# First attention of a two-block transformer kernel: values held stationary for two heads in the two column halves of the array, probabilities scaled ahead of their transposes

## The chip, the cores and the metric

The kernel runs on one core of a Trainium2 chip. The metric is the device time of one execution in microseconds (us). TensorE is the matrix engine: a matmul loads its stationary operand into a 128 x 128 array and streams the moving operand through it, a column at a time. VectorE (DVE in the profile), ScalarE (ACT) and GpSimd (POOL) are the other compute engines, each with an instruction stream of its own that is worked off in order; they meet at semaphores. SyncE (SP) issues the loads.

## The reference

The reference is two transformer blocks on 256 tokens of width 1024. The first block is a feed-forward part, a mixing part and a second feed-forward part; the second block has a differential attention, a recurrence and an MLP. What the change touches is the mixing part of the first block, in which two attentions of 8 heads of width 64 run side by side over the same normed input `u`:

```
qa, ka, va, qb, kb, vb, qi, ki, wi, g = jnp.split(u @ w_in[l], SPLIT_POINTS, axis=-1)
...
out_a = dsa_attention(qa, ka, va, qi, ki, wi, bias_dsa)
out_b = moba_attention(qb, kb, vb, bias_moba)
...
mixed = g_a * (out_a @ w_branch_dsa[l]) + g_b * (out_b @ w_branch_moba[l])
h = h + mixed @ w_out[l]
```

Both are causal softmax attentions with a bias by distance; with 256 tokens `moba_attention` has a single block and is plain causal attention. `dsa_attention` lets each query see only the 64 keys with the highest scores of a small index network:

```
_, idx = lax.top_k(scores, topk)
...
p = jax.nn.softmax(logits, axis=-1)
return jnp.einsum('bqhk,bqkhd->bqhd', p.astype(v.dtype), v_sel)
```

## The kernel before

Weights are streamed from memory in units of 128 x 4 x 512 numbers through a ring of three buffers. Each unit is split into two parts, `hi` (ScalarE, L721 for half a unit in this stage, L712 for a whole one elsewhere) and `lo` (VectorE, L1135 or L1118), and each product of activations and weights is done as three matmuls of 512 moving columns, at L1635 to L1637. A call of `portion` is four such threes, 12 matmuls.

The mixing part's input products are 11 chunks of columns (`IN1`), two units and two tiles of 128 tokens each, so 44 portions. The program counts them as positions p = 0 to 43, and each engine's instruction stream walks through the same positions in its own loop `for p in range(4 * len(IN1))`. Tables by position say where an engine fits in the attention's work: TensorE does the portion of position p and then the small matmuls that the tables put there. Of the table `M1_STEP` an entry is the position at which a head's logits are made, one step for each of 16 heads: steps k = 0 to 7 are the heads of the `moba` attention, 8 to 15 those of the `dsa` attention.

```
M1_STEP = [17, 19, 21, 22, 23, 24, 25, 26] + [29 + k for k in range(NH)]
```

For step k with s = M1_STEP[k]:

- TensorE at s, for even k: `pair_scores`, the scores of two heads, with their 64 rows of queries and keys in the upper and lower half of the array's rows (L1781 to L1785).
- VectorE at s: `logits` (L1258), which adds the bias and finds the maximum of each row, into `l1[:, k % 4]`. 384 columns: 256 keys for the second tile of queries, 128 for the first, since the first can't see later keys.
- ScalarE at s + 1: the exponential, with row sums (L929), semaphore `m_p`.
- TensorE at s + 3: three transposes of 128 x 128 into the bank `PT` (L1868), which wait for `m_p`.
- ScalarE at s + 3: the copy from `PT` to `pt1` (L897).
- TensorE at s + 4: the values product (L1882 to L1884), three matmuls with the transposed probabilities stationary and 64 columns of values moving.

When a branch's 8 heads are done, VectorE takes reciprocals of the sums and scales the outputs from the banks `O` into `hid` (L1426); TensorE then transposes them tile by tile at the positions `M1_OUT_T` (L1894), and ScalarE and VectorE split what comes out into `mth` and `mtl`, or `ath` and `atl` (L937, L1434), the stationary operands of the branch's output product.

Other work stands between these on VectorE. At each of the positions 13 to 20 it does an eighth of the search for the top keys (L1405 to L1408); at 21 the found keys become a mask (L1411). Queries and keys of the chunks 4 and 5 (positions 16 to 23) are normed: VectorE sums squares of each head (L1343, L1345), GpSimd takes the root (`head_rstd`, L633), VectorE scales (`head_scale`, L1351), one position after the sums, and TensorE transposes the result (L1837). GpSimd, after its last root, adds the mask to the `dsa` bias in one instruction (L650, `bias_a<-bias_a,score`). At each position VectorE ends with half a split (L1135).

## Time and profile before

| | |
|---|---|
| median of 3 runs | 1036.5 us (1035.03 to 1036.72) |
| the profiled execution | 1035.49 us |
| its span, first to last instruction | 1033.7 us |
| TensorE busy | 1021.1 us, 99% of the span |
| VectorE busy | 626.5 us, 61% |
| ScalarE busy | 544.6 us, 53% |
| GpSimd busy | 121.7 us, 12% |
| first attention, 250 to 356 us: TensorE, VectorE, ScalarE busy | 104.19, 76.35 and 63.30 us |

Times of rows are microseconds from the span's start. Matmuls are pipelined, so the time from the start of one to the start of the next is its price, not the duration in its row, which overlaps with the next one's.

### The profile page before, as it was taken

How to read it: one execution, taken by the hardware profiler on the slowest of the kernel's cores; microseconds unless marked ns; L12 is line 12 of the kernel's file. 1: busy time of each engine (PE TensorE's matmuls, PEld its weight loads, DVE VectorE, ACT ScalarE, POOL GpSimd, SP SyncE). 2: the span in 40 equal slices, each digit the busy share in tenths (PEclk: the TensorE clock that was granted, in tenths of full speed). 3: DMA queues.
4: the chain of work that ended last, by engine and by line, in shares of the span. 5: the costliest groups of instructions: out<-in, count | busy, mean ns of one | idle time of the engine just before them, and what ended most of it. 6: DMA issues, size and time to landing. Idle time of an engine off the chain costs nothing.

```text
span 1033.7 us, 13217 instructions
## 1 busy us (share of the span) xinstructions
PE 1021.1 (99%) x4854; PEld 840.3 (81%) x4854; DVE 626.5 (61%) x868; ACT 544.6 (53%) x745; POOL 121.7 (12%) x110
## 2 busy tenths in 40 slices
PE   8999999999999999999999999999999999999998
PEld 6788888888878888888888888888888888888886
DVE  5555454568875667554454667766498765454553
ACT  7344434565755636444434576766875555444441
POOL 0000000032310000000000041219913000000000
PEclk9999999999999999999999999999999999999999
DMA  7777665585433546656555366445355555555541
GB/s 248 240 242 241 203 232 188 161 295 181 143 122 124 172 153 204 202 166 201 175 191 192 134 248 206 151 135 163 122 188 197 185 163 198 174 199 175 190 162 41
DMA packets 113815, 188.83 MB, mean 183 GB/s; under 512 B 4577, under 2 KB 60010, under 8 KB 113642
## 3 DMA queue, kind: packets, MB, share of 16 engines
q1 hardware_dynamic: 113754, 188.23, 55.2%
q8 instruction: 28, 0.46, 0.2%
q14 instruction: 17, 0.14, 0.0%
q10 hardware_dynamic: 16, 0.00, 0.0%
HBM read 182.45 MB, written 5.77 MB: 182 GB/s over the span
## 4 chain that ended last, share of the span: by engine, by line
PE 91%; DVE 3%; ACT 2%; DMA 1%; POOL 1%; issue 1%; SPq 1%; DVEq 0%; ACTq 0%; POOLq 0%
PE bank L1635 21%; PE bank L1637 21%; PE bank L1636 21%; PE bank L1730 7%; PE bank L1729 7%; PE bank L1731 6%; PE bank L1674 2%; PE bank L1647 1%; PE bank L1781 1%; DVE hid L1351 1%; ACT hi L712 1%; DVE lo L1135 1%; POOL rstd_q L633 1%; PE bank L1971 1%; DMA resid<-in_x 1%
## 5 line engine op out<-in xcount | busy, mean ns | idle before, releaser
L1635 PE MATMUL bank<-hi,xh 128*128 128x512 f32 (+1 forms) x944 | 378.2, 401 | 2.4 <-DVE hid L1171 0.8
L1637 PE MATMUL bank<-hi,xl 128*128 128x512 f32 (+1 forms) x944 | 368.1, 390 | 0.0
L1636 PE MATMUL bank<-lo,xh 128*128 128x512 f32 (+1 forms) x944 | 366.6, 388 | 0.0
L1118 DVE TENSOR_TENSOR lo<-raw,hi 128x2048 fp32r<-128x2048 f32 x112 | 255.9, 2286 | 174.5 <-ACT hi L712 174.4
L712 ACT ACTIVATE hi<-raw 128x2048 fp32r<-128x2048 f32 (+1 forms) x116 | 220.6, 1903 | 141.7 <-PE bank L1731 98.6
L1635 PEld LDWEIGHTS bank<-hi,xh 128*128 128x128 f32 x944 | 177.4, 188 | 39.9 <-DVE xl L1157 1.8
L1637 PEld LDWEIGHTS bank<-hi,xl 128*128 128x128 f32 x944 | 177.2, 188 | 37.9
L1636 PEld LDWEIGHTS bank<-lo,xh 128*128 128x128 f32 x944 | 177.7, 188 | 33.6
L1135 DVE TENSOR_TENSOR lo<-raw,hi 128x1024 fp32r<-128x1024 f32 (+1 forms) x108 | 133.2, 1242 | 53.6 <-ACT hi L721 53.0
L1729 PE MATMUL bank<-hi,hh 128*128 128x512 f32 x304 | 119.7, 394 | 1.1 <-DVE hl L1181 1.1
L1730 PE MATMUL bank<-lo,hh 128*128 128x512 f32 x304 | 119.7, 394 | 0.0
L1731 PE MATMUL bank<-hi,hl 128*128 128x512 f32 x304 | 118.2, 389 | 0.0
L721 ACT ACTIVATE hi<-raw 128x1024 fp32r<-128x1024 f32 x100 | 104.0, 1050 | 13.1 <-PE bank L1637 9.9
L789 ACT ACTIVATE hh<-bank 128x512 fp32r<-128x512 f32 x38 | 21.9, 597 | 115.2 <-PE bank L1674 115.2
L1729 PEld LDWEIGHTS bank<-hi,hh 128*128 128x128 f32 x304 | 57.1, 188 | 14.1 <-issue 1.3
L1731 PEld LDWEIGHTS bank<-hi,hl 128*128 128x128 f32 x304 | 57.1, 188 | 12.8
L1181 DVE TENSOR_TENSOR hl<-bank,hh 128x512 fp32r<-128x512 f32 x38 | 25.5, 688 | 68.8 <-ACT hh L789 68.8
L1730 PEld LDWEIGHTS bank<-lo,hh 128*128 128x128 f32 x304 | 57.2, 188 | 11.3
L626 POOL TENSOR_TENSOR small<-small 128x1 f32<-128x1 f32 x10 | 8.2, 822 | 377.4 <-DVE small L1142 377.4
L633 POOL TENSOR_TENSOR rstd_q<-ss_q,small 128x8 f32<-128x8 f32 x16 | 37.8, 2362 | 92.5 <-DVE ss_q L1345 92.5
L778 ACT ACTIVATE act_out<-bank,small 128x256 f32<-128x256 f32 x44 | 20.8, 474 | 50.4 <-PE bank L1637 50.4
L1171 DVE SCALAR_TENSOR_TENSOR hid<-bank,small,act_out 128x256 f32<-128x256 f32 x44 | 21.1, 481 | 18.1 <-ACT act_out L778 18.1
(247 smaller groups left out, 941.3 us busy)
## 6 DMA issues: line engine op xcount, KB each, us to landing
raw<-in_w_in SPq DMA_DIRECT2D x48, 1024.0 KB
raw<-in_ffn_w_gu SPq DMA_DIRECT2D x84, 512.0 KB
raw<-in_ffn_w_down SPq DMA_DIRECT2D x22, 1024.0 KB
raw<-in_w_up SPq DMA_DIRECT2D x16, 1024.0 KB
raw<-in_w_down SPq DMA_DIRECT2D x16, 1024.0 KB
raw<-in_w_out SPq DMA_DIRECT2D x8, 1024.0 KB
distance_table<-ftab SPq DMA_DIRECT2D x8, 576.0 KB
raw<-in_w_proj_attn SPq DMA_DIRECT2D x4, 1024.0 KB
```

The source lines that it names most:

```text
L633: nc.gpsimd.tensor_tensor(rstd_q[:, s], ss_q[:, s], minus_half[:, 0:8], ALU.pow).then_inc(rstd_sem, 1)
L712: nc.scalar.activation(hi[s][:, :, 0:width], raw[s][:, :, 0:width], ACT.Copy).then_inc(hi_done, 1)
L721: ins = nc.scalar.activation(hi[s][:, cut, :], raw[s][:, cut, :], ACT.Copy)
L1118: nc.vector.tensor_tensor(lo[s][:, :, 0:width], raw[s][:, :, 0:width], hi[s][:, :, 0:width].bitcast(F32), ALU.subtract).then_inc(lo_done, 1)
L1135: ins = nc.vector.tensor_tensor(lo[s][:, cut, 0:width], raw[s][:, cut, 0:width], hi[s][:, cut, 0:width].bitcast(F32), ALU.subtract)
L1181: nc.vector.tensor_tensor(hl[:, kt:kt + 2, :], X[b][:, :].rearrange("p (k c) -> p k c", k=2), hh[:, kt:kt + 2, :].bitcast(F32), ALU.subtra ...
L1635: nc.tensor.matmul(o, sh, wh, start=first and j == 0, stop=False)
L1636: nc.tensor.matmul(o, sh, wl, start=False, stop=False)
L1637: ins = nc.tensor.matmul(o, sl, wh, start=False, stop=last and j == 3)
L1729: nc.tensor.matmul(DB[t][h][:, :], sh, wh, start=begin, stop=False)
L1730: nc.tensor.matmul(DB[t][h][:, :], sh, wl, start=False, stop=False)
L1731: ins = nc.tensor.matmul(DB[t][h][:, :], sl, wh, start=False, stop=end)
```

## The change

Three things change together. The probabilities of a step are scaled by their reciprocal sums in `l1`, by VectorE at position s + 2, ahead of the transposes, which now wait for that (semaphore `m_n`) and not for the exponential. The values product is done once for two heads (`pair_values`): a head's values, 64 columns, are stationary, one head in the left column half of the array and the other in the right, and the transposed probabilities move, 256 and 128 columns; it comes out with the features in the partitions, as the output product wants it. So the scaling and the transposes of outputs go, and ScalarE and VectorE split the outputs straight from the banks `O`, four heads at a time, at the positions `M1_OUT`. `pt1` has four buffers in place of two.

```diff
-M1_OUT_T = [32, 33, 42, 43]
+M1_OUT = [27, 31, 37, 41]
...
-            pt1 = sb("pt1", [P, 2, SPAN], F32, s)
+            pt1 = sb("pt1", [P, 4, SPAN], F32, s)
...
                     act.wait_ge(m_pt, k + 1)
-                    if k >= 2:
-                        act.wait_ge(m_pv, k - 1)
-                    nc.scalar.activation(pt1[:, k % 2, :], PT[:, 0:SPAN], ACT.Copy).then_inc(m_ptc, 1)
+                    if k >= 4:
+                        act.wait_ge(m_pv, k - 3)
+                    nc.scalar.activation(pt1[:, k % 4, :], PT[:, 0:SPAN], ACT.Copy).then_inc(m_ptc, 1)
...
-                j = at(M1_OUT_T, p)
+                j = at(M1_OUT, p)
                 if j >= 0:
-                    act.wait_ge(m_ot, j + 1)
+
+                    act.wait_ge(m_pv, 4 * (j + 1))
                     dst = mth if j < 2 else ath
-                    nc.scalar.activation(dst[:, :, j % 2 * P:(j % 2 + 1) * P],
-                                         X[0][:, :].rearrange("p (k c) -> p k c", c=P), ACT.Copy).then_inc(m_oh, 1)
+                    nc.scalar.activation(dst[:, 2 * (j % 2):2 * (j % 2) + 2, :],
+                                         O[j % 2][:, :].rearrange("p (k c) -> p k c", c=SEQ),
+                                         ACT.Copy).then_inc(m_oh, 1)
...
-                for branch in range(2):
-                    if M1_STEP[NH * branch + NH - 1] + 4 == p:
-
-                        dve.wait_ge(m_p, NH * (branch + 1))
-                        cut = slice(2 * NH * branch, 2 * NH * (branch + 1))
-                        step(nc.vector.reciprocal(inv[:, cut], sums[:, cut]))
-                        dve.wait_ge(m_pv, NH * (branch + 1))
-                        if branch == 0:
-                            dve.wait_ge(m_tr, 10)
-                        else:
-                            dve.wait_ge(m_ot, 2)
-                        for tt in range(NT):
-                            r = inv[:, cut].rearrange("p (h q) -> p h q", q=2)[:, :, 1 - tt:2 - tt]
-                            nc.vector.tensor_tensor(hid[:, tt, :].rearrange("p (h c) -> p h c", c=HD),
-                                                    O[tt][:, :].rearrange("p (h c) -> p h c", c=HD),
-                                                    r.to_broadcast([P, NH, HD]), ALU.mult).then_inc(m_o, 1)
-                j = at(M1_OUT_T, p)
+                k = at(M1_STEP, p - 2)
+                if k >= 0:
+
+                    dve.wait_ge(m_p, k + 1)
+                    step(nc.vector.reciprocal(inv[:, 2 * k:2 * k + 2], sums[:, 2 * k:2 * k + 2]))
+                    for q, cut in enumerate((slice(0, SEQ), slice(SEQ, SPAN))):
+                        ins = nc.vector.tensor_scalar(l1[:, k % 4, cut], l1[:, k % 4, cut],
+                                                      inv[:, 2 * k + q:2 * k + q + 1], None, ALU.mult)
+                    ins.then_inc(m_n, 1)
+                j = at(M1_OUT, p)
                 if j >= 0:
                     dve.wait_ge(m_oh, j + 1)
...
+            def pair_values(v, k):
+
+                h = k % NH
+                o = O[h // 4]
+                first = h // 2 % 2 * SEQ
+                whole, late = slice(first, first + SEQ), slice(first + P, first + SEQ)
+                left, right = slice(h * HD, h * HD + HD), slice(h * HD + HD, h * HD + 2 * HD)
+                one, two = pt1[:, k % 4, :], pt1[:, k % 4 + 1, :]
+                nc.tensor.matmul(o[0:HD, whole], v[:, 0, left], one[:, 0:SEQ], start=True, stop=False)
+                nc.tensor.matmul(o[HD:P, whole], v[:, 0, right], two[:, 0:SEQ], start=True, stop=False)
+                nc.tensor.matmul(o[0:HD, late], v[:, 1, left], one[:, SEQ:SPAN],
+                                 start=False, stop=True).then_inc(m_pv, 1)
+                nc.tensor.matmul(o[HD:P, late], v[:, 1, right], two[:, SEQ:SPAN],
+                                 start=False, stop=True).then_inc(m_pv, 1)
...
                 k = at(M1_STEP, p - 3)
                 if k >= 0:
 
-                    pe.wait_ge(m_p, k + 1)
+                    pe.wait_ge(m_n, k + 1)
                     if k >= 1:
                         pe.wait_ge(m_ptc, k)
-                    for j in range(3):
-                        ins = nc.tensor.transpose(PT[:, j * P:(j + 1) * P], l1[:, k % 4, j * P:(j + 1) * P],
+                    for j, b in enumerate((2, 0, 1)):
+                        ins = nc.tensor.transpose(PT[:, j * P:(j + 1) * P], l1[:, k % 4, b * P:(b + 1) * P],
                                                   ident[:, :])
                     ins.then_inc(m_pt, 1)
                 k = at(M1_STEP, p - 4)
-                if k >= 0:
+                if k >= 0 and k % 2 == 1:
+
                     pe.wait_ge(m_ptc, k + 1)
-                    if k == 0:
+                    if k == 1:
                         pe.wait_ge(m_ev, 8)
-                    if k == NH:
-                        pe.wait_ge(m_o, 2)
+                    if k == NH + 1:
                         pe.wait_ge(m_ev, 14)
...
+                    if k >= NH and k % 4 == 1:
+                        pe.wait_ge(m_ol, (k - NH) // 4 + 1)
+                    pair_values(v1 if k < NH else v1b, k - 1)
...
-                    if q == 2:
-                        pe.wait_ge(m_ol, 3 + t)
+                    if q in (0, 2) and t == 0:
+                        pe.wait_ge(m_ol, q + 2)
```

The order of instructions shows it at three places. On TensorE, behind the portion of position 21: the transposes of normed queries, the scores of two heads, and before the change the values product of step 0.

```order
L1837 MATMUL bank<-ident,hid 128x128 [waits m_qn,m_trev]
L1837 MATMUL bank<-ident,hid 128x128 x3
L1781 MATMUL bank<-k_m,q_m 128x256 [waits m_l]
L1782 MATMUL bank<-k_m,q_m 128x256
L1783 MATMUL bank<-k_m,q_m 128x128
L1785 MATMUL bank<-k_m,q_m 128x128
L1882 MATMUL bank<-v,pt 128x64 [waits m_ev,m_ptc]
L1883 MATMUL bank<-v,pt 128x64
L1884 MATMUL bank<-v,pt 128x64
```

After the change the first values product stands two positions later, behind the portion and the scores of position 23, and is that of the steps 0 and 1; its outputs are 64 partitions high (`64x256`, `64x128`).

```order
L1775 MATMUL bank<-k_m,q_m 128x256 [waits m_l]
L1776 MATMUL bank<-k_m,q_m 128x256
L1777 MATMUL bank<-k_m,q_m 128x128
L1779 MATMUL bank<-k_m,q_m 128x128
L1790 MATMUL bank<-pt,v 64x256 [waits m_ev,m_ptc]
L1791 MATMUL bank<-pt,v 64x256
L1792 MATMUL bank<-pt,v 64x128
L1794 MATMUL bank<-pt,v 64x128
```

So the single product went from position 21, and a pair's came at 23. The transposes of step 0, at position 20, stand where they stood, and wait for `m_n` in place of `m_p`.

On VectorE at position 19, with the end of the head sums, a part of the top-key search, and the split, before the change:

```order
L1345 TENSOR_SCALAR ss_q<-ss_q 128x8 [waits m_red]
L1405 MAX small<-score 128x8
L1406 MAX small<-score 128x8
L1407 MATCH_REPLACE score<-small,score 128x256 [waits dve_step]
L1408 MATCH_REPLACE score<-small,score 128x128
L1135 TENSOR_TENSOR lo<-raw,hi 128x1024 [waits hi_half,dve_step]
L1351 TENSOR_TENSOR hid<-hid,rstd_q 128x512 [waits m_rstd]
```

and after it:

```order
L1346 TENSOR_SCALAR ss_q<-ss_q 128x8 [waits m_red]
L1406 MAX small<-score 128x8
L1407 MAX small<-score 128x8
L1408 MATCH_REPLACE score<-small,score 128x256 [waits dve_step]
L1409 MATCH_REPLACE score<-small,score 128x128
L1418 RECIPROCAL small<-small 128x2 [waits m_p,dve_step]
L1420 TENSOR_SCALAR l<-l,small 128x256 [waits dve_step]
L1420 TENSOR_SCALAR l<-l,small 128x128
L1136 TENSOR_TENSOR lo<-raw,hi 128x1024 [waits hi_half]
L1352 TENSOR_TENSOR hid<-hid,rstd_q 128x512 [waits m_rstd]
```

The scaling of step 0 (L1418, L1420) stands between the search and the split.

On VectorE at position 24, where the logits of step 5 are followed by the last head scaling, before the change:

```order
L1262 TENSOR_SCALAR small<-small 128x2 [waits dve_step]
L1351 TENSOR_TENSOR hid<-hid,rstd_q 128x512 [waits m_rstd]
L1135 TENSOR_TENSOR lo<-raw,hi 128x1024 [waits hi_done]
L1258 ISA l,small<-bank,bias_m 128x256 [waits m_pt,m_s]
L1258 ISA small 128x1
```

and after it:

```order
L1263 TENSOR_SCALAR small<-small 128x2 [waits dve_step]
L1352 TENSOR_TENSOR hid<-hid,rstd_q 128x512 [waits m_rstd]
L1418 RECIPROCAL small<-small 128x2 [waits m_p]
L1420 TENSOR_SCALAR l<-l,small 128x256 [waits dve_step]
L1420 TENSOR_SCALAR l<-l,small 128x128
L1136 TENSOR_TENSOR lo<-raw,hi 128x1024 [waits hi_done]
L1259 ISA l,small<-bank,bias_m 128x256 [waits m_pt,m_s]
L1259 ISA small 128x1
```

The scaling of step 3 stands directly behind the head scaling. TensorE's transposes of step 3 are at position 25.

## Rows read from the trace of the kernel before

**Rows 1.** The page: TensorE's share of the span, and its granted clock in 40 slices.

```profile
PE 1021.1 (99%) x4854; PEld 840.3 (81%) x4854; DVE 626.5 (61%) x868; ACT 544.6 (53%) x745; POOL 121.7 (12%) x110
...
PEclk9999999999999999999999999999999999999999
```

**Rows 2.** TensorE's waits: line, releaser, us in total, times, longest.

```profile
PE bank L1837 <- DVE hid L1351: 1.8, 1, 1.8
```

**Rows 3.** Timeline of TensorE around a values product alone: start, duration, line, tiles.

```profile
345.23 0.39 PE L1637 MATMUL bank<-hi,xl 128*128 128x512 f32 x1
...
346.59 0.39 PE L1637 MATMUL bank<-hi,xl 128*128 128x512 f32 x1
```

**Rows 4.** The same around the transposes L1894 of an output tile.

```profile
351.36 0.40 PE L1637 MATMUL bank<-hi,xl 128*128 128x512 f32 x1
...
352.50 0.40 PE L1637 MATMUL bank<-hi,xl 128*128 128x512 f32 x1
```

**Rows 5.** The same around a scores product of two heads.

```profile
309.11 0.39 PE L1637 MATMUL bank<-hi,xl 128*128 128x512 f32 x1
309.42 0.48 PE L1781 MATMUL bank<-k_a,q_a 64*128 64x256 f32 x1
309.43 0.48 PE L1782 MATMUL bank<-k_a,q_a 64*128 64x256 f32 x1
...
309.96 0.27 PE L1783 MATMUL bank<-k_a,q_a 64*128 64x128 f32 x1
...
310.07 0.27 PE L1783 MATMUL bank<-k_a,q_a 64*128 64x128 f32 x1
...
310.85 0.40 PE L1637 MATMUL bank<-hi,xl 128*128 128x512 f32 x1
```

**Rows 6.** Timeline of ScalarE at position 18: the exponential of step 0.

```profile
260.54 0.51 ACT L929 ACTIVATE l<-l,small 128x256 f32<-128x256 f32 x1
```

**Rows 7.** Timeline of TensorE: transposes of steps 0, 2 and 3, then L1837.

```profile
263.12 0.49 PE L1868 MATMUL bank<-ident,l 128*128 128x128 f32 x3
...
279.13 0.49 PE L1868 MATMUL bank<-ident,l 128*128 128x128 f32 x3
...
283.60 0.55 PE L1868 MATMUL bank<-ident,l 128*128 128x128 f32 x3
...
289.40 0.63 PE L1837 MATMUL bank<-ident,hid 128*128 128x128 f32 x4 [1.81 <-DVE hid L1351]
```

**Rows 8.** Timeline of VectorE: splits of positions 19 and 22, then 23 and 24.

```profile
267.29 1.22 DVE L1135 TENSOR_TENSOR lo<-raw,hi 128x1024 fp32r<-128x1024 f32 x1
...
275.94 1.22 DVE L1135 TENSOR_TENSOR lo<-raw,hi 128x1024 fp32r<-128x1024 f32 x1 [0.56 <-ACT hi L721]
277.09 0.42 DVE L1258 CUSTOM_DVE_ANT_0 l<-bank,bias_m 128x256 f32<-128x256 f32 x1
...
277.83 0.68 DVE L1351 TENSOR_TENSOR hid<-hid,rstd_q 128x512 f32<-128x512 f32 x1
...
279.15 0.17 DVE L1345 TENSOR_SCALAR ss_q<-ss_q 128x8 f32<-128x8 f32 x1
...
281.97 7.28 DVE L1351 TENSOR_TENSOR hid<-hid,rstd_q 128x512 f32<-128x512 f32 x1 [0.77 <-POOL rstd_q L633]
```

**Rows 9.** Timeline of VectorE in the second attention: a reciprocal and two multiplications.

```profile
640.17 0.17 DVE L1508 RECIPROCAL small<-small 128x4 f32<-128x4 f32 x1
...
640.64 0.55 DVE L1513 TENSOR_SCALAR l<-l,small 128x256 f32<-128x256 f32 x2
```

**Rows 10.** Timeline of GpSimd: the last root of head sums and the mask addition.

```profile
279.40 2.54 POOL L633 TENSOR_TENSOR rstd_q<-ss_q,small 128x8 f32<-128x8 f32 x1 [2.30 <-DVE ss_q L1345]
281.91 6.79 POOL L650 TENSOR_TENSOR bias_a<-bias_a,score 128x3072 f32<-128x3072 f32 x1
```

**Rows 11.** Timeline of TensorE at the start of the trace, 0 to 14 us.

```profile
1.82 1.97 PE L1768 MATMUL bank<-ident 128*128 128x128 f32 x8 [1.82 <-POOL small L621]
...
5.67 2.35 PE L1768 MATMUL bank<-ident 128*128 128x128 f32 x20
```

More of the change, by code:

```diff
@@ L352, in program @@
         m_p = sem("m_p")
+        m_n = sem("m_n")
         m_pt = sem("m_pt")
@@ L355, in program @@
         m_pv = sem("m_pv")
-        m_o = sem("m_o")
-        m_ot = sem("m_ot")
         m_oh = sem("m_oh")
@@ L1432, in _ @@
                     hi_, lo_ = (mth, mtl) if j < 2 else (ath, atl)
-                    cut = slice(j % 2 * P, (j % 2 + 1) * P)
-                    nc.vector.tensor_tensor(lo_[:, :, cut], X[0][:, :].rearrange("p (k c) -> p k c", c=P),
-                                            hi_[:, :, cut].bitcast(F32), ALU.subtract).then_inc(m_ol, 1)
+                    cut = slice(2 * (j % 2), 2 * (j % 2) + 2)
+                    nc.vector.tensor_tensor(lo_[:, cut, :], O[j % 2][:, :].rearrange("p (k c) -> p k c", c=SEQ),
+                                            hi_[:, cut, :].bitcast(F32), ALU.subtract).then_inc(m_ol, 1)
                 mixing_split(split_lo_half, U_M1, p)
@@ L1871, in _ @@
                 k = at(M1_STEP, p - 4)
-                if k >= 0:
+                if k >= 0 and k % 2 == 1:
                     pe.wait_ge(m_ptc, k + 1)
-                    if k == 0:
+                    if k == 1:
                         pe.wait_ge(m_ev, 8)
-                    if k == NH:
-                        pe.wait_ge(m_o, 2)
+                    if k == NH + 1:
                         pe.wait_ge(m_ev, 14)
-                    h = k % NH
-                    v = v1 if k < NH else v1b
-                    cut = slice(h * HD, (h + 1) * HD)
-                    nc.tensor.matmul(O[1][:, cut], pt1[:, k % 2, 0:P], v[:, 0, cut], start=True, stop=False)
-                    nc.tensor.matmul(O[1][:, cut], pt1[:, k % 2, P:SEQ], v[:, 1, cut], start=False, stop=True)
-                    nc.tensor.matmul(O[0][:, cut], pt1[:, k % 2, SEQ:SPAN], v[:, 0, cut],
-                                     start=True, stop=True).then_inc(m_pv, 1)
-                j = at(M1_OUT_T, p)
-                if j >= 0:
-                    pe.wait_ge(m_o, j + 1)
-                    if j == 0:
-                        pe.wait_ge(m_trev, 10)
-                    else:
-                        pe.wait_ge(m_ol, j)
-                    for b in range(4):
-                        ins = nc.tensor.transpose(X[0][:, b * P:(b + 1) * P], hid[:, j % 2, b * P:(b + 1) * P],
-                                                  ident[:, :])
-                    ins.then_inc(m_ot, 1)
+                    if k >= NH and k % 4 == 1:
+                        pe.wait_ge(m_ol, (k - NH) // 4 + 1)
+                    pair_values(v1 if k < NH else v1b, k - 1)
             for q in range(4):
```

## The prediction

> **What bounds the kernel now.** The page says TensorE is busy for 99% of the span [rows 1], and its list of waits has only a few entries: 1.8 us is its wait in the first attention, the transposes at L1837 waiting for a VectorE instruction [rows 2]. So I read the first attention as a timeline of TensorE between 250 and 356 us, and beside it the timelines of VectorE, ScalarE and GpSimd. The reader should look for two things: what a small group of matmuls costs between two long ones, and when each small group would be ready to run under its new wait. As TensorE has nothing spare, every microsecond that it loses or saves in this stage should be in the end time.
>
> **Prices on TensorE.** Long matmuls follow each other every 0.227 us. Three of them, with the thing between, give each price. With one head's values: 345.23 to 346.59 is 1.36, less 0.68 for the three, 0.68 us a head [rows 3]. With four transposes of outputs: 351.36 to 352.50 is 1.14, so 0.46 [rows 4].
>
> The new values product, one for a pair of heads, is in no row. Its nearest is the scores product of a pair, which has the same shape turned round: 256 and 128 moving columns for two heads, in two row halves of the array. From 309.11 to 310.85 it costs 1.06 us [rows 5]. The two heads' rows start 0.01 us apart, so the halves run together; one pass over 128 columns takes 0.11 (309.96 to 310.07), so one over 256 takes about 0.21, two passes each, which is 0.64 of streaming; the other 0.42 goes at the edges. I take 1.06. The bounds are 0.64 (no edges) and 1.70 (the column halves run one behind the other, 0.64 more).
>
> The Trainium skill, TensorEngine Tiling (Array Packing), section Tiling Modes, says that a change of tiling mode drains the array, which speaks against small excursions into column halves. The 0.42 at the edges of the row-half product would be that drain, and it is in my 1.06; without it a pair would cost 0.64, by the bound above. The same page has column halves as independent tiles that work in parallel, which no row here shows.
>
> **What is removed and added on TensorE.** Sixteen values products go, 16 x 0.68 = 10.9. Eight pair products come, 8 x 1.06 = 8.5. Net -2.4. The four groups of output transposes go, 4 x 0.46 = -1.8. That is -4.2 us of work. The transposes of probabilities stay as many as they were.
>
> **The new wait.** Before, the transposes of step k wait for the exponential alone (m_p). Now they wait for VectorE's scaling (m_n), which VectorE runs at its position STEP+2, while TensorE wants it at the end of its position STEP+3. That is enough only if VectorE is no more than a position behind. It isn't, in the stretch with the top-key search.
>
> Step 0. The exponential begins at 260.54 on ScalarE, with some 0.9 us of work in its two parts [rows 6]; TensorE's transposes ran at 263.12 [rows 7]. In VectorE's order the scaling of step 0 now stands behind the position-19 part of the top-key search, in front of the split that began at 267.29 [rows 8]. It costs, by the like instructions of the second attention, 0.17 us for the reciprocal at 640.17 and 0.55 for the two multiplications at 640.64, with the gaps for the two handovers 0.8 us together [rows 9]. It is ready at 268.1, and TensorE starts 0.1 later: 268.2 instead of 263.12, **5.1 us idle**. VectorE doesn't need TensorE's position 20 for anything it does until then, so nothing moves forward. Queued behind the waiting transposes is the whole of TensorE's work; ScalarE's copy of step 0, and with it the exponential of step 1 and a split, wait too, but at position 20 ScalarE had time (copy, exponential and split are some 2.3 us of work, done by 271, when VectorE's own work ahead of that split ends).
>
> Step 1. Everything on TensorE now comes 5.1 - 0.68 = 4.4 later than before, since the values product of step 0 is gone from position 21. VectorE, behind the scores product of position 21, has the logits of step 2 (0.74), a mask (0.3) and the scaling of step 1 (0.8) to do, 1.9 us; TensorE has a whole position, 12 x 0.227 = 2.7 us, and four transposes in the same time. No wait.
>
> Step 2. ScalarE in position 22 hangs on TensorE's transposes of that position and is 4.4 late with them. So VectorE's split of position 22, which waited for ScalarE and began at 275.94, begins at 280.3; from there VectorE works without a gap: head sums of position 23, which ended at 279.2, end at 283.6, and the scaling of step 2 at 284.4. TensorE comes at 279.13 + 4.4 + 0.4 (a pair product in place of a single one) = 283.9. **0.6 us idle** [rows 7, 8].
>
> Step 3. Here is the second large one. As soon as the last root of head sums is done, GpSimd starts the mask addition, 6.79 us, and VectorE's head scaling that starts 0.06 us later takes 7.28 us instead of the 0.68 of its like at 277.83: it gets nowhere until GpSimd is finished [rows 8, 10]. In VectorE's new order the scaling of step 3 stands right behind that blocked instruction. Sums at 283.6, root 2.54 us, addition 6.79, 0.5 from its end to that of the blocked instruction: VectorE comes free at about 293.5, and its scaling of step 3 is done at 294.3. TensorE is at these transposes at 283.60 + 4.4 + 0.4 + 0.6 = 289.0 and starts them at 294.4. **5.4 us idle**. The old 1.8 us at 289.40 vanishes, because TensorE now comes to L1837 at 297.8, long after.
>
> Later steps. Steps 4 to 7 have slack of 1 to 3 us (step 4: scaled at 297.0, wanted at 298.2). Step 8 is the closest: logits, a gate addition of much the same length (0.74) and 0.8 of scaling behind the scores product of position 31, 2.3 in all, against one position of 2.7 us on TensorE, 0.4 us of slack. The outputs, taken straight from the banks at positions 27, 31, 37 and 41, are three positions or more ahead of whoever wants them. The new instructions on VectorE outside these places (12 scalings, 9.6 us) are hidden by its idle time, and what goes from it frees nothing. The loads and the splits run some four positions ahead and are only pushed along.
>
> **Sum.** -2.4 - 1.8 + 5.1 + 0.6 + 5.4 - 1.8 = **+5.1 us**.
>
> **The clock.** In the middle of this kernel TensorE is never idle for 5 us; the wait at L1837 is 1.8 [rows 2]. At the start of the trace, after TensorE's first idle time, eight transposes take 1.97 us, 0.25 each, and a little later twenty of the same take 2.35 us, 0.12 each [rows 11]: half the pace, from 1.82 to 5.67 at most, although the granted clock is in the top tenth in every slice of the page, which is its 2.4 GHz level [rows 1]. If a stall of 5 us throws TensorE back to that, it loses half of about 3.9 us, 2.0 us for each of the two stalls. I take one of the two: +2.0, with 0 and 4.0 as bounds. The Trainium skill, TensorE: Matmul & The Clock Gate, Part 1, says that the half rate is what an idle array falls back to and that sustained activity lifts it.
>
> So **+7.1 us** on the profiled execution's 1035.49, 1042.6. The median of the runs, 1036.5, is 1.0 above that execution, which gives **1043.5**.
>
> **The rivals.**
> *The column halves don't run together* (17%). A pair costs 1.70: 8 x 0.64 = 5.1 more, of which the first 0.6 falls into the wait at step 2. +9.6 without the clock, +13.6 with both drops: 1046 to 1050. For it: no matmul of this trace has two column halves, and both halves need all 128 rows of their own moving data, where the row halves shared them. Against: the row halves do run together.
> *The second stall doesn't come* (14%), the one on the other side. If the head scaling of position 24 gets in ahead of GpSimd's mask addition, or the addition doesn't block it, VectorE has step 3 scaled before 289.0 and nothing waits there; the old 1.8 goes all the same. -2.4 - 1.8 + 5.1 + 0.6 - 1.8 = -0.3, or +1.7 with a clock drop, 1036 to 1038, and with pair products at the lower bound (0.64, 3.4 less in all) 1033. It decides at 289.0: VectorE must be free by 288.2. Against: GpSimd started its addition in the same 0.1 us in which the root ended, which leaves VectorE no time to be told.
> *VectorE is slower still* (9%): the scaling itself blocked or lengthened beside GpSimd, so that step 8 or the steps 4 to 7 wait too, half a us each: 1046 to 1049.
> *The forecast*, overlap and both stalls, has 60%: 1041.6 with no drop of the clock to 1045.6 with two.
>
> **How the numbers follow.** About 0.2%, 2.1 us, is what a measurement of this kernel can tell. The forecast and the two slow rivals are slower, 86%; of the 14% I give 8 to no change and 6 to faster. The range leaves out most of the rival at 1036 and the last of the one at 1050: 1038 to 1049.5.
>
> **What would show it.** In the changed kernel's waits TensorE should have some 5 us at the first transposes of probabilities and again some 5 us at the fourth, both on VectorE's scaling, and nothing at L1837. A VectorE head scaling of 7 us beside GpSimd's addition should be there as before. The eight pair products should cost about 1.06 by the rows on either side, with both halves starting together. Wrong would be: a first wait under 3 us (then VectorE's backlog was not what I read), pair products near 1.7, or long matmuls of 0.45 us spacing for more than 4 us behind a stall.

## The result, and the profile after

| | before | after |
|---|---|---|
| median of 4 runs on one chip | 1035.76 us (1034.85 to 1036.72) | 1042.74 us (1041.62 to 1044.02) |
| profiled execution: span | 1033.7 us | 1040.5 us |
| profiled execution: its own time | 1035.49 us | 1042.31 us |

The change makes the kernel slower: the ratio of the times is 1.0068, with a 95% interval from 1.0050 to 1.0085. The forecast was 1043.5.

The page of the changed kernel, the rows that answer to [rows 1]:

```profile
PE 1021.4 (98%) x4806; PEld 835.7 (80%) x4806; DVE 633.1 (61%) x910; ACT 544.7 (52%) x745; POOL 120.8 (12%) x110
...
PEclk9999999999989999999999999999999999999999
```

TensorE is busy as long as before with 48 instructions less, so some of them must have run longer, and its granted clock has one slice out of forty below the top tenth, the one from 286 to 312 us, in the first attention. Where it waits now stands in its waits (line, releaser, us in total, times, longest), the rows that answer to [rows 2]:

```profile
PE bank L1877 <- DVE l L1420: 5.4, 2, 4.8
PE bank L1775 <- DVE small L1263: 4.1, 1, 4.1
PE bank L1762 <- POOL small L620: 1.8, 1, 1.8
```

Two waits are new, 9.5 us in all. (L1762 is at the start and was there before [rows 11]; in the changed kernel the three matmuls of a portion are L1629 to L1631, the transposes of probabilities L1877, of queries and keys L1846, the scores L1775 to L1779, VectorE's scaling L1418 and L1420.) The old wait of 1.8 us at the transposes of queries and keys [rows 2] is gone. TensorE's timeline behind the first wait (start, duration, line, tiles; in brackets the wait ahead of it):

```profile
267.91 0.90 PE L1877 MATMUL bank<-ident,l 128*128 128x128 f32 x3 [4.83 <-DVE l L1420]
269.04 0.63 PE L1630 MATMUL bank<-lo,xh 128*128 128x512 f32 x1
269.46 0.63 PE L1631 MATMUL bank<-hi,xl 128*128 128x512 f32 x1
...
271.56 0.40 PE L1631 MATMUL bank<-hi,xl 128*128 128x512 f32 x1
271.80 0.39 PE L1629 MATMUL bank<-hi,xh 128*128 128x512 f32 x1
...
272.49 0.60 PE L1846 MATMUL bank<-ident,hid 128*128 128x128 f32 x4
```

The reader is to see two things. The wait is 4.83 us on VectorE's scaling of step 0. And behind it the same long matmuls that follow each other every 0.23 us from 271.6 on are 0.42 apart: about half the pace. From these transposes to the next at L1846 it takes 4.58 us (267.91 to 272.49). In the kernel before the same work took 3.09, from 263.12 [rows 7] to this row:

```profile
266.21 0.60 PE L1837 MATMUL bank<-ident,hid 128*128 128x128 f32 x4
```

And around the second:

```profile
293.40 0.79 PE L1775 MATMUL bank<-k_m,q_m 64*128 64x256 f32 x1 [4.05 <-DVE small L1263]
...
294.98 0.90 PE L1877 MATMUL bank<-ident,l 128*128 128x128 f32 x3
...
299.68 0.49 PE L1846 MATMUL bank<-ident,hid 128*128 128x128 f32 x3
```

VectorE and GpSimd at that time, from their timelines:

```profile
286.61 0.42 DVE L1259 CUSTOM_DVE_ANT_0 l<-bank,bias_m 128x256 f32<-128x256 f32 x1
...
287.29 6.06 DVE L1263 TENSOR_SCALAR small<-small 128x2 f32<-128x2 f32 x1
293.26 0.68 DVE L1352 TENSOR_TENSOR hid<-hid,rstd_q 128x512 f32<-128x512 f32 x1
```

```profile
284.99 1.64 POOL L632 TENSOR_TENSOR rstd_q<-ss_q,small 128x8 f32<-128x8 f32 x1 [2.67 <-DVE ss_q L1346]
286.59 6.72 POOL L649 TENSOR_TENSOR bias_a<-bias_a,score 128x3072 f32<-128x3072 f32 x1
```

GpSimd's mask addition ends at 293.31. VectorE's instruction at L1263, on 128 x 2 numbers, takes 0.17 us elsewhere and 6.06 here. The scores of position 25 wait for it, since they go into the bank that the logits in front of it read.

The clock is read from the windows (stretch, length, busy time and instructions of each engine, granted clock, share and rate of the DMA):

```profile
266.00:270.00 4.00, 2.09 (x7) 1.80 (x8) 3.90 (x13) 1.15 (x4) 1.49 (x1) 0.70 0.50 194
270.00:274.00 4.00, 4.00 (x23) 3.14 (x22) 2.12 (x7) 2.03 (x5) 0.00 (x0) 0.87 0.15 15
...
290.00:294.00 4.00, 0.60 (x4) 0.52 (x6) 4.00 (x3) 0.07 (x1) 3.32 (x1) 0.69 0.00 0
294.00:300.00 6.00, 6.00 (x26) 4.80 (x23) 4.77 (x17) 2.31 (x6) 0.00 (x0) 0.64 0.53 170
```

In both places it is the 1.2 GHz level that pulls the mean of a window below 1.00. Read in windows of 1 us it is 0.50 from 268 to 271 and again from 292 to 298.

A product of a pair of values, the one thing that no row before had shown:

```profile
315.23 0.39 PE L1631 MATMUL bank<-hi,xl 128*128 128x512 f32 x1
315.55 0.43 PE L1790 MATMUL bank<-pt,v 128*64 128x256 f32 x1
315.55 0.43 PE L1791 MATMUL bank<-pt,v 128*64 128x256 f32 x1
315.81 0.38 PE L1790 MATMUL bank<-pt,v 128*64 128x256 f32 x1
...
316.93 0.40 PE L1631 MATMUL bank<-hi,xl 128*128 128x512 f32 x1
```

Both column halves start at 315.55, so they run together. The next pass starts 0.26 later, and from one L1631 to the next it is 1.70 us; less 0.68 for the three long matmuls, a pair costs 1.02.

**The account of the span.** New waits 4.83 + 0.62 + 4.05 = +9.5. The old wait -1.8. The slow clock: 1.5 behind the first wait (4.58 - 3.09), 2.3 behind the second (6.28 from 293.40 to 299.68; the same work takes 3.99, from 282.97 to 286.96, in b2 below, where nothing waits in it), +3.8. The work saved, -4.4 by the runs b2 and b3 below (-4.2 by the prediction). That makes +7.1; the spans differ by 6.8.

### The profile page after: what moved, and what is told of

Its sections match the earlier page's. It is cut to its first block, busy times and chain, and to the rows that moved or that the text cites. A ratio compares the mean times of both kernels' runs of the same rounds, so it can differ in the third digit from the quotient of the medians.

```text
span 1040.5 us, 13156 instructions
## 1 busy us (share of the span) xinstructions
PE 1021.4 (98%) x4806; PEld 835.7 (80%) x4806; DVE 633.1 (61%) x910; ACT 544.7 (52%) x745; POOL 120.8 (12%) x110
## 4 chain that ended last, share of the span: by engine, by line
PE 92%; DVE 3%; ACT 2%; DMA 1%; issue 1%; SPq 1%; POOL 0%; DVEq 0%; ACTq 0%
PE bank L1629 22%; PE bank L1631 21%; PE bank L1630 21%; PE bank L1723 7%; PE bank L1724 7%; PE bank L1725 6%; PE bank L1668 2%; PE bank L1775 1%; PE bank L1641 1%; ACT hi L711 1%; PE bank L1965 1%; DMA resid<-in_x 1%; DVE small L1263 1%; PE bank L1877 1%; SPq L479 0%
## 5 line engine op out<-in xcount | busy, mean ns | idle before, releaser
L1629 PE MATMUL bank<-hi,xh 128*128 128x512 f32 (+1 forms) x944 | 379.4, 402 | 2.1 <-DVE xl L1158 0.8
L1631 PE MATMUL bank<-hi,xl 128*128 128x512 f32 (+1 forms) x944 | 368.8, 391 | 0.0
L1629 PEld LDWEIGHTS bank<-hi,xh 128*128 128x128 f32 x944 | 178.2, 189 | 41.2 <-issue 2.4
L1631 PEld LDWEIGHTS bank<-hi,xl 128*128 128x128 f32 x944 | 177.7, 188 | 38.1
L1725 PEld LDWEIGHTS bank<-hi,hl 128*128 128x128 f32 x304 | 57.1, 188 | 12.9
```

Of the source, the lines that this page charges most:

```text
L1629: nc.tensor.matmul(o, sh, wh, start=first and j == 0, stop=False)
L1631: ins = nc.tensor.matmul(o, sl, wh, start=False, stop=last and j == 3)
L1725: ins = nc.tensor.matmul(DB[t][h][:, :], sl, wh, start=False, stop=end)
```

## The experiments

The theory: all of the loss is two waits, both set by the place of the new scaling in VectorE's order and the second by GpSimd's mask addition, plus the clock that falls behind them; the products themselves are a gain. The rivals: the pair products, or their switch to column halves, cost what is lost; the scaling lengthens VectorE's work as such; the clock costs nothing.

The first four are edits of the changed kernel and ran on one chip, where the kernel before took 1035.22 us. The other four shared another, with the kernel before at 1035.15. The changed kernel's 1042.74 is from the runs of the result, with the kernel before at 1035.76, and was not taken again on these two chips. Two of its four executions have a mean clock of 0.995, as the profiled one, and average 1041.97 us; the two at 0.993 average 1043.60. So a difference from 1042.74 can be off by a microsecond, and the table at the end of this section gives the first attention alone, from the profiled executions.

**a1_no_scaling: the pair products alone.**

```diff
-                    dve.wait_ge(m_p, k + 1)
-                    step(nc.vector.reciprocal(inv[:, 2 * k:2 * k + 2], sums[:, 2 * k:2 * k + 2]))
-                    for q, cut in enumerate((slice(0, SEQ), slice(SEQ, SPAN))):
-                        ins = nc.vector.tensor_scalar(l1[:, k % 4, cut], l1[:, k % 4, cut],
...
-                    pe.wait_ge(m_n, k + 1)
+                    pe.wait_ge(m_p, k + 1)
```

> The changed kernel without VectorE's scaling of the probabilities; TensorE's transposes wait for the exponential again. It leaves out the division by the sums, so its outputs are not the reference's. What is left of the change is its work on TensorE: 8 pair products for 16 single ones and no transposes of outputs. Theory (the time is lost to waits on the scaling and to the clock behind them): no wait on VectorE's scaling, no fall of the clock, only the old wait at the transposes of normed keys, 1.8 to 3 us; 4 to 5 us faster than the kernel before, so about 1031.5. Rival (products in the column halves are dear themselves, by changes of mode or slower streams): no faster than the kernel before, 1036 or more.

Measured: 1031.88 us, ratio 0.9971 (0.9962 to 0.9981), 3.3 faster than before and within 0.4 of the 1031.5 expected. TensorE's waits at the transposes of probabilities are gone, and the one at the transposes of queries and keys is back, a little longer, as its timeline and the window around it show; another of 0.51 us has come at the scores of position 21 (276.08), which TensorE now reaches sooner.

```profile
291.00 1.09 PE L1837 MATMUL bank<-ident,hid 128*128 128x128 f32 x4 [2.64 <-DVE hid L1352]
```

```profile
290.00:294.00 4.00, 3.00 (x15) 2.12 (x15) 3.97 (x9) 1.87 (x4) 0.31 (x1) 0.62 0.20 30
```

So the pair products and the missing output transposes are a gain, and the rival that they cost the time has fallen. Even behind 2.64 us of waiting the granted clock fell in this execution, which took 1035.16 us and had another fall at 14 to 17 us, near the start; the mean clock of five of the nine executions was 1.00.

**a2_busy_waits: TensorE kept busy while it waits.** 38 transposes of the identity into a free bank ahead of the transposes of step 0, 32 ahead of the scores of position 25.

```diff
+            def idle_work(count):
+                for _ in range(count):
+                    nc.tensor.transpose(bank[5][:, 0:P], ident[:, :], ident[:, :])
...
+                    if k == 6:
+                        idle_work(32)
...
+                    if k == 0:
+                        idle_work(38)
```

> The changed kernel with TensorE given idle work in its two long waits: 38 transposes of the identity into a free bank ahead of the first transposes of probabilities, 32 ahead of the scores of position 25. At 0.12 us each they fill 4.5 and 3.8 us, less than the waits of 4.8 and 4.1. Theory (the clock falls because TensorE is idle, and costs 1.5 us behind the first wait and 2.1 behind the second): granted clock 1.00 throughout, 3.0 to 3.6 us faster than the changed kernel, 1039. Rival (the fall is an accident of where the waits lie, or costs nothing at the end): no difference from the changed kernel, 1042.7.

Measured: 1038.84 us, ratio 1.0033 (1.0021 to 1.0045), 3.9 less than the changed kernel's 1042.74. The fillers in TensorE's timeline, and the windows of both places:

```profile
263.02 4.31 PE L1767 MATMUL bank<-ident 128*128 128x128 f32 x38
```

```profile
266.00:270.00 4.00, 3.32 (x24) 2.80 (x22) 3.90 (x13) 1.41 (x6) 1.58 (x1) 1.00 0.54 207
...
294.00:300.00 6.00, 6.00 (x35) 4.69 (x34) 4.38 (x18) 5.11 (x14) 0.00 (x0) 1.00 0.55 175
```

TensorE gains nothing useful by this work. Its transposes of step 0 start 14.16 us after its first scores product, exactly as in the changed kernel, since VectorE is ready no sooner; but the clock stays at 1.00. So the fall of the clock costs time, and that rival has fallen. How much it costs is better read from the first attention alone (the table below), where the profiled executions differ by 3.2 us and not by 3.9. That is 0.6 less than the 3.8 of the account, and most of the rest has gone into waits: TensorE, faster again, waits 9.9 us in all here, the idle work counted as waiting, in place of 9.5, 0.33 of it at the transposes behind the scores of position 25, where it had no wait at the slow clock.

**a3_whole_array: no column halves.** Two heads' values stand in all 128 columns and both heads' probabilities are streamed through them one behind the other, so a pair costs twice the streaming and never leaves the whole array. The outputs are sums over two heads, not the reference's.

```diff
-                nc.tensor.matmul(o[0:HD, whole], v[:, 0, left], one[:, 0:SEQ], start=True, stop=False)
-                nc.tensor.matmul(o[HD:P, whole], v[:, 0, right], two[:, 0:SEQ], start=True, stop=False)
+                both = slice(h * HD, h * HD + 2 * HD)
+                nc.tensor.matmul(o[:, whole], v[:, 0, both], one[:, 0:SEQ], start=True, stop=False)
+                nc.tensor.matmul(o[:, whole], v[:, 0, both], two[:, 0:SEQ], start=False, stop=False)
...
```

> The changed kernel with each pair product done in the whole array in place of its halves: the values of both heads, 128 columns, are stationary, and the probabilities of one head and of the other stream through them one behind the other. The outputs of a head are then mixed with those of its neighbour, so they are not the reference's. Theory (the column halves stream together): each pair product streams 0.64 us longer and saves at most 0.3 at its edges, 8 x 0.4 to 8 x 0.64, 3 to 5 us slower than the changed kernel. Rival (the halves take turns in truth, or a change of mode costs as much as they save): within 1 us of the changed kernel.

Measured: 1044.92 us, ratio 1.0089 (1.0074 to 1.0104), 2.2 above the changed kernel, less than the 3 to 5 expected. TensorE's timeline of one pair, behind three transposes:

```profile
308.92 0.40 PE L1631 MATMUL bank<-hi,xl 128*128 128x512 f32 x1
309.16 0.49 PE L1878 MATMUL bank<-ident,l 128*128 128x128 f32 x3
...
311.26 0.40 PE L1631 MATMUL bank<-hi,xl 128*128 128x512 f32 x1
```

2.34 us in all, less 0.68 for the long matmuls and 0.34 for the transposes, is 1.32 for the pair against 1.02 in halves. Eight times 0.30 is 2.4, and the first attention alone is 2.4 longer than the changed kernel's. Halving the streaming from 1.28 to 0.64 saved only 0.3, because some 0.4 goes at the edges of the product in halves and next to nothing at those of the whole one.

**a4_mask_in_eight: the mask addition in eight pieces.**

```diff
-            nc.gpsimd.tensor_tensor(bias_a[:, :, :], bias_a[:, :, :],
-                                    score[:, :].unsqueeze(1).to_broadcast([P, NH, SPAN]),
+            for h in range(NH):
+                nc.gpsimd.tensor_tensor(bias_a[:, h, :], bias_a[:, h, :], score[:, :],
...
-                    if k == NH:
-                        dve.wait_ge(m_masked, 1)
+                    if k >= NH:
+                        dve.wait_ge(m_masked, k - NH + 1)
```

> The changed kernel with GpSimd's mask addition cut into eight, one for each head, so that VectorE can get in between. Theory (the second wait is VectorE held by that one instruction of 6.7 us): VectorE's small instruction at its start takes under 1.2 us in place of 6.1, TensorE's wait of 4.1 us at the scores of position 25 and the fall of the clock behind it (2.1 us) are gone, 5 to 6 us faster than the changed kernel, about 1037. Rival (GpSimd takes the port again at once and keeps VectorE out, or VectorE would be late anyway): the wait stays above 3 us and the time within 1 us of the changed kernel.

Measured: 1037.9 us, ratio 1.0021 (1.0012 to 1.0030), 4.8 less than the changed kernel. TensorE's waits in the first attention, then GpSimd's and VectorE's timelines:

```profile
PE bank L1877 <- DVE l L1420: 6.6, 3, 4.8
```

```profile
287.94 9.39 POOL L650 TENSOR_TENSOR bias_a<-bias_a,score 128x384 f32<-128x384 f32 x8
```

```profile
289.50 0.15 DVE L1418 RECIPROCAL small<-small 128x2 f32<-128x2 f32 x1
289.69 1.86 DVE L1420 TENSOR_SCALAR l<-l,small 128x256 f32<-128x256 f32 x2
291.47 2.04 DVE L1136 TENSOR_TENSOR lo<-raw,hi 128x1024 fp32r<-128x1024 f32 x1
```

The wait at the scores is gone, as VectorE's instruction at L1263 takes 0.36 us; 1.16 has come back at the transposes of step 3, behind a slower scaling. Waits are 2.9 us less, and the second fall of the clock, 2.3, went with them, 5.2 together; the first attention alone became 4.7 shorter, and the other 0.5 has no place in the account. The two engines now take turns between pieces, and both are slower for it: the addition takes 9.39 us instead of 6.72, the scaling pair 1.86 instead of 0.55, the split 2.04 instead of 1.22. Only the reciprocal keeps its 0.15.

**b1_scaling_sooner: the scaling one position earlier on VectorE,** at STEP+1, behind the logits and ahead of the split.

```diff
-                k = at(M1_STEP, p - 2)
+                k = at(M1_STEP, p - 1)
```

> The changed kernel with VectorE's scaling one position sooner, at STEP+1 in place of STEP+2, at the end of the position's work and ahead of its split. VectorE waits there for ScalarE anyway: 1.1 us ahead of the split of position 18, since ScalarE makes that split's first half behind the exponential. Theory (the first wait is nothing but the place of the scaling in VectorE's order): scaling of step 0 done at 262.2, before TensorE wants it at 263.1; no wait at steps 0 and 2, no fall of the clock there. The mask addition still holds VectorE, and TensorE waits 2 to 3.5 us once at positions 25 or 26. About 1033, 9 to 10 us faster than the changed kernel and 2 to 3 faster than the kernel before. Rival (scaling ahead of the transposes always costs its wait, as VectorE then waits for ScalarE and is late with the rest): 1038 or more.

Measured: 1036.65 us, ratio 1.0016 (1.0007 to 1.0025): 6 less than the changed kernel, but not the 9 to 10 expected. The first wait is gone and the transposes of probabilities are no longer in the list of waits, but the second has stayed, and 0.76 has come at the scores of position 21 (274.53), as TensorE's waits and timeline show:

```profile
PE bank L1775 <- DVE small L1263: 5.7, 2, 4.9
```

```profile
287.67 0.71 PE L1775 MATMUL bank<-k_m,q_m 64*128 64x256 f32 x1 [4.93 <-DVE small L1263]
```

```profile
281.58 6.04 DVE L1263 TENSOR_SCALAR small<-small 128x2 f32<-128x2 f32 x1
```

GpSimd starts its addition at 280.88 and VectorE is held at L1263 for 6.04 us, and TensorE, itself some 6 us earlier, comes to the same scores in the middle of it. The account: waits 9.5 to 5.7, -3.8; the clock 3.8 to 1.6 (from 287.67 to the next L1846 at 293.28, 5.61 against 3.99), -2.2; together -6.0. My expectation had the addition still in the way, but for 2 to 3.5 us of TensorE's time and with no fall of the clock behind it; it was 4.93, with a fall. So the second wait doesn't hang on the scaling standing late. It does need the scaling somewhere ahead of those logits: in the kernel before and in a1, which has no scaling, VectorE is done with L1263 (L1262 before) when the addition starts, the instruction held is the head scaling (7.28 us [rows 8], and 7.23 in a1), and TensorE waits at L1837 (1.81 and 2.64) and not at the scores.

**b2_sooner_and_spread: both,** and each piece of the addition waits until the logits of a later step are made, so that GpSimd's work is spread over eight positions.

```diff
+            for h in range(NH):
+                pool.wait_ge(m_l, h + 5)
+                nc.gpsimd.tensor_tensor(bias_a[:, h, :], bias_a[:, h, :], score[:, :],
...
+                    if k >= NH:
+                        dve.wait_ge(m_masked, k - NH + 1)
...
-                k = at(M1_STEP, p - 2)
+                k = at(M1_STEP, p - 1)
```

> As the run with the scaling one position sooner, and the mask addition cut into eight, each piece started when the logits of one more step are done (from step 4 on), so that VectorE is held for under 1 us once in a position. Theory: no wait of TensorE over 1 us and granted clock 1.00 in the whole attention; 2.5 to 5 us faster than with the scaling sooner alone, about 1029. Rival (pieces hold VectorE as long in sum, so the wait only moves to the steps 8 to 15): 1032 or more.

Measured: **1029.52 us**, ratio 0.9946 (0.9932 to 0.9960), faster than both kernels. It computes all of the reference, and every scaling is there, so the rival that the scaling costs by its mere work on VectorE has fallen too. TensorE's only wait in the first attention, two of GpSimd's rows of pieces, and a window of it:

```profile
PE bank L1776 <- DVE small L1264: 0.8, 1, 0.8
```

```profile
281.18 2.50 POOL L651 TENSOR_TENSOR bias_a<-bias_a,score 128x384 f32<-128x384 f32 x2
286.01 1.02 POOL L651 TENSOR_TENSOR bias_a<-bias_a,score 128x384 f32<-128x384 f32 x1 [2.32 <-DVE small L1264]
```

```profile
286.00:290.00 4.00, 4.00 (x26) 3.05 (x26) 3.20 (x8) 3.13 (x9) 1.67 (x2) 1.00 0.80 262
```

And the scores of position 25 with the next transposes of queries and keys, 3.99 us apart, which is the price at full clock of the work that stands behind the changed kernel's second wait:

```profile
282.97 0.48 PE L1776 MATMUL bank<-k_m,q_m 64*128 64x256 f32 x1
...
286.96 0.60 PE L1847 MATMUL bank<-ident,hid 128*128 128x128 f32 x4
```

**b3_before_spread: the kernel before, with the spread addition alone.** The same edit as above, without the last two lines.

> The kernel before with nothing but the mask addition in eight pieces, each started when the logits of one more step are done. It tells how much of the gain of the run with both belongs to the values product. Theory: the wait of 1.8 us at the transposes of normed keys goes, 1 to 2 us faster than the kernel before; the new values product is then worth the remaining 4 to 5. Rival (the addition in pieces costs VectorE more than it frees): no difference.

Measured: 1033.09 us, ratio 0.9983 (0.9974 to 0.9992), 2.1 faster than before. TensorE has no wait left in the first attention. This is the partner for b2: neither has the waits in question, and the change is 3.6 us faster there (1029.52 against 1033.09). With b2's own wait of 0.8 added, that is 4.4 of saved work, where the prediction had 4.2.

**b4_scaling_alone: the kernel before, with the scaling and its wait alone.** The probabilities are scaled ahead of their transposes by the changed kernel's code; products and transposes stay as before. The outputs are multiplied by the reciprocals a second time.

```diff
+                k = at(M1_STEP, p - 2)
+                if k >= 0:
+                    dve.wait_ge(m_p, k + 1)
...
-                    pe.wait_ge(m_p, k + 1)
+                    pe.wait_ge(m_n, k + 1)
```

> The kernel before with the scaling ahead of the transposes alone, at STEP+2, and TensorE's transposes waiting for it; values products, outputs and their transposes as before. The outputs are scaled a second time, so they are not the reference's. Theory (the waits come from the place of the scaling and not from the new products): waits of about 5, 0.5 and 4 to 5 us on VectorE, the clock down behind the two long ones, 9 to 12 us slower than the kernel before, 1045 to 1047. Rival (the waits belong to the pair products, whose place has moved): under 5 us slower.

Measured: 1047.66 us, ratio 1.0116 (1.0100 to 1.0131), 12.5 slower than before, a little over the 9 to 12 expected. TensorE's waits have the same lines, releasers and sizes as in the changed kernel:

```profile
PE bank L1877 <- DVE l L1420: 5.9, 3, 4.8
PE bank L1790 <- DVE small L1263: 4.1, 1, 4.1
```

So the waits belong to the scaling, and not to the pair products. The clock behind the second lasts longer here, as TensorE's timeline shows, in which a long matmul still takes 0.63 us (0.39 at full clock) 7 us behind it:

```profile
294.26 0.48 PE L1790 MATMUL bank<-k_m,q_m 64*128 64x256 f32 x1 [4.06 <-DVE small L1263]
...
301.34 0.63 PE L1644 MATMUL bank<-hi,xh 128*128 128x512 f32 x1
...
302.37 0.60 PE L1846 MATMUL bank<-ident,hid 128*128 128x128 f32 x4
```

From 294.26 to 302.37 is 8.1 us. At full clock it would be 4.0, as in b2, and 0.7 for the values product of one head [rows 3] that stands there in this kernel alone; 0.3 is a wait that is counted already. The fall costs the other 3.1. The account: waits 5.9 + 4.1, the old wait -1.8, the clock 1.6 (267.96 to 272.67, less 3.09) + 3.1, together +12.9; the spans differ by 13.0 (1046.7 against 1033.7). a1 and b4 are the change taken apart: -3.3 and +12.5 make +9.2, 2.2 more than the +7.0 of both. The accounts say where, with 2.7 a little too much: a1's waits (2.64 and 0.51) are 1.3 longer than the old one, and in b4 the clock takes 0.9 and the waits 0.5 more than in the changed kernel.

**The first attention alone.** In each profiled execution, from TensorE's first scores product (`bank<-k_m,q_m`) to its first long matmul of the other branch's output product (`bank<-hi,ath`). This leaves out the start of the kernel, where the clock fell at 13 to 17 us in the profiled executions of a1, a3, a4 and b3 and not in the others, and it doesn't depend on the chip's median.

| | from, to (us) | length | against before |
|---|---|---|---|
| before | 253.94, 366.25 | 112.3 | |
| changed | 253.75, 372.97 | 119.2 | +6.9 |
| a1 | 255.36, 365.86 | 110.5 | -1.8 |
| a2 | 253.85, 369.83 | 116.0 | +3.7 |
| a3 | 255.02, 376.60 | 121.6 | +9.3 |
| a4 | 254.93, 369.43 | 114.5 | +2.2 |
| b1 | 253.23, 366.58 | 113.4 | +1.0 |
| b2 | 253.52, 360.24 | 106.7 | -5.6 |
| b3 | 255.37, 365.70 | 110.3 | -2.0 |
| b4 | 253.80, 379.21 | 125.4 | +13.1 |

## Why the prediction was right, step by step

- **Pair products 1.06.** Measured 1.02 alone (315.23 to 316.93), and 0.80 where it stands right behind scores, which are in halves too (280.01 to 282.55 is 2.54, less 0.68 and 1.06). Both halves start together; the rival that they don't has fallen. Taken from the nearest row of the same shape turned round [rows 5], the price was right to 0.04, its edges included.
- **The saved work, -4.2.** Shown by b2 against b3, 3.6, or 4.4 with b2's wait. The two terms of it, values and output transposes, were not measured apart.
- **First wait, 5.1.** Measured 4.83 (4.8 in b4 too). TensorE started at 267.91, I had 268.2. Shown by b1, which moved nothing but the scaling and lost this wait.
- **Step 2, 0.6.** Measured 0.62.
- **Second wait, 5.4 at the transposes of step 3.** This step named the wrong waiter. VectorE came free at 293.3, where I had 293.5, and GpSimd was the cause as said. But the instruction held was L1263, right behind the logits, and not the head scaling at L1352, which I said would take its 7 us as before: it took 0.68. So TensorE stopped already at the scores of position 25, which stand ahead of the transposes in its order, and waited 4.05. I had followed only the new semaphore. The old one, of the scores on the logits, passes through the same blocked engine. a4 shows the addition in one piece as the cause, b1 that the scaling's late place isn't needed for it, and a1 that without any scaling the wait falls at L1837 instead. The size was off by two things. I took the last root at 2.54 us as in [rows 10], and it took 1.64 (284.99), which brings the addition 0.9 sooner; why it is shorter is not shown. And at full clock TensorE would have waited a little again at the transposes (0.33 in a2), which the slow clock hid. That VectorE came free nearly when I said is luck: the root was 0.9 shorter, and the sums ended at 284.9 where I had 283.6, since I added the clock at the end and didn't carry it through the times of both engines.
- **The old wait, -1.8.** Gone, as said.
- **Later steps, no wait.** Right: no other row of waits is in this stage, step 8 with its 0.4 us of slack included, so the rival of a VectorE that is slower still has fallen.
- **The clock, +2.0 with 0 and 4.0 as bounds.** The term was mis-sized: I took one fall out of two, there were two. The 2.0 for each was near (1.5 and 2.3); the account has 3.8 for both, and keeping the clock up gave back 3.2 in a2. One of my signs of being wrong came half true: behind the second wait the half pace lasted from 293.40 to 298.24, 4.8 us, though only the last 2.7 of them were long matmuls. The missing 1.8 made up for a second wait that was 1.35 shorter than predicted and a first that was 0.3 shorter; the total hit the mark by errors of opposite sign. (My sum, 1036.5 and 7.1, is 1043.6; I wrote 1043.5.)
- **The rival on the other side,** that the second stall doesn't come, would have needed VectorE free by 288.2. It was free at 293.3.

The Trainium skill, SBUF — State Buffer, section SBUF: two separate sides, says that VectorE and GpSimd share a pair of ports and that whoever comes first holds it for a whole instruction, against VectorE instructions in a two-port mode or with two inputs in SBUF. The traces here agree: L1263 lost 5.9 us and the logits at L1259, which have one of their inputs in a bank, ran in their usual 0.42 in the first half microsecond of the same addition. In which mode L1263 ran no row here shows.

What stays open: why the slow matmuls behind a wait of 4.1 us go on for 5 us in the changed kernel and to 7 us behind it in b4, where the clock fell only at 295, after the wait had ended at 294.26, and in the changed kernel by 292, in the middle of it; why the last root took 1.64 us and not 2.54; and what a pair product costs apart from its neighbours in all eight places.

## What to carry to other kernels

When a producer on another engine is put between two steps, place it by the last moment at which its engine is really free, in the longest stretch of that engine's program, and not by how many positions it has in a table: here one position earlier was worth 6 us. When one engine is held by another's long instruction, list every semaphore that passes through the held engine; the one that stops TensorE is the first in TensorE's order, not the one that was added. And price a stall of TensorE with the slow stretch behind it: waits of 4 to 5 us cost 1.5 to 3.1 us more.

## What the runs showed of the hardware that was not expected

- The granted clock fell to its 1.2 GHz level behind much shorter waits than the two of 4 to 5 us: behind 2.64 us in a1, and in the profiled execution of b3 behind 1.94 us near the start; TensorE's timeline there:

```profile
13.43 0.66 PE L1648 MATMUL bank<-ident,resid 128*128 128x128 f32 x4 [1.94 <-DMA resid<-in_x]
...
14.31 0.63 PE L1637 MATMUL bank<-lo,xh 128*128 128x512 f32 x1
```

  The kernel before had 2.3 us in one wait on the same load without a fall, and a2 2.5. Executions of b3 with a mean clock of 1.00 took 1032.8 to 1033.1 us, those with 0.998, as the profiled one, 1034.4 to 1035.1: about 2 us for one fall.
- A GpSimd instruction of 6.7 us holds even a VectorE instruction on 128 x 2 numbers until it ends (6.06 and 6.04 us instead of 0.17).
- Cutting that GpSimd instruction into eight costs GpSimd 2.7 us (9.39 against 6.72) when VectorE works between the pieces.
- A product in column halves pays some 0.4 us at its edges, one in the whole array next to nothing, so that half the streaming saved 0.3 us a pair and not 0.6.
- Transposes of the identity kept the granted clock at 1.00 over both long waits: 38 of them (4.31 us) and 32 (3.66 us) in a2.
